# FFN1's down projection runs sub-block by sub-block, and the mixer's first buffers move to the upper part of the shared region

## The reference, cut to what matters

```
def layer_forward(x, ...):            # x: prompt 2048 x 1024, sample 128 x 1024 per core
    x = x + 0.5 * swiglu(rmsnorm(x, g1), w_gate, w_up, w_down)      # FFN1, D_FF = 2816
    h = rmsnorm(x, g2)
    u_lru, gate, u_pool = split(h @ w_in)                          # 512 + 512 + 512
    u_conv = causal_conv(u_lru, width 4);  hs = rglru(u_conv)      # gates, then a scan over time
    y = concat(gelu(gate) * hs, pool_mixer(u_pool)) ; x = x + y @ w_out
    x = x + cross_attend(rmsnorm(x, g3), mem_k, mem_v)
    x = x + 0.5 * swiglu(rmsnorm(x, g4), ...)                       # FFN2, same sizes
```

## Time and profile before

| | |
|---|---|
| runs of before | 1868.54 and 2052.18 us (median 1960.36) |
| the profiled execution | 1870.9 us, span 1869.1 us on core 1 |
| spans of the 8 cores | 1852.7 to 1869.1 us, granted clock 0.896 to 0.903 |
| TensorE (PE) busy | 1517.2 us, 81% of the span |
| VectorE (DVE), ScalarE (ACT), GpSimd (POOL) busy | 697, 509, 254 us |
| POOL's DMA queue | 142.36 MB written, 68.9% of 16 engines' span |

### The profile page before, as it was taken

One profiled execution on the slowest core, in us unless ns is written; L12 is line 12 of the kernel. 1 busy time (PEld: TensorE's weight loads), 2 busy tenths in 40 slices (PEclk: granted clock), 3 DMA queues, 4 the chain that ended last, 5 costly groups with the idle time before them and its releaser, 6 DMA issues.

```text
span 1869.1 us, 23927 instructions; the slowest of 8 cores (1852.7 to 1869.1 us)
## 1 busy us (share of the span) xinstructions
PE 1517.2 (81%) x8564; PEld 761.6 (41%) x8564; DVE 696.9 (37%) x1121; ACT 508.5 (27%) x914; POOL 253.5 (14%) x305
## 2 busy tenths in 40 slices
PE   4799997548868999886999998475675589999975
PEld 3344443225323444344455554133334444555334
DVE  3312116665275121145322114767553144222223
ACT  3211114463313111133111112573433332111111
POOL 4011101002000112210011100011102100112220
PEclk8899999778989999998999999797796599999996
DMA  9376956577913779994355953597949933558996
GB/s 173 39 82 70 108 62 72 56 96 95 134 50 41 76 83 86 118 185 96 46 68 69 99 60 44 58 113 82 124 59 144 166 46 46 69 68 80 126 159 110
DMA packets 344633, 166.20 MB, mean 89 GB/s; under 512 B 164787, under 2 KB 330675, under 8 KB 344502
## 3 DMA queue, kind: packets, MB, share of 16 engines
q0 software_dynamic: 337584, 142.36, 68.9%
q1 hardware_dynamic: 6934, 22.30, 3.8%
HBM read 295.54 MB, written 11.67 MB: 164 GB/s over the span
## 4 chain that ended last, share of the span: by engine, by line
PE 66%; DMA 12%; DVE 12%; ACT 5%; issue 4%; DVEq 0%; SPq 0%; ACTq 0%; POOLq 0%
PE psb L341 64%; DMA ring<-f2d 4%; DMA regA<-cv 4%; DVE regA L812 3%; DVE hT L470 2%; DVE rstd L463 2%; DMA yp<-regA 2%; DMA ring<-wq 1%; DVE regA L722 1%; DVE xT L466 1%; PE psb L916 1%; ACT hT L452 1%; DMA stg<-spool 1%; PE psb L936 1%; DMA ring<-win 1%
## 5 line engine op out<-in xcount | busy, mean ns | idle before, releaser
L341 PE MATMUL psb<-hT,ring 128*128 128x512 bf16 (+1 forms) x4960 | 948.9, 355 | 119.6 <-DVE hT L737 41.4
L341 PEld LDWEIGHTS psb<-hT,ring 128*128 128x128 bf16 x4960 | 451.5, 100 | 614.3 <-issue 166.6
L341 PE MATMUL psb<-regA,ring 128*128 128x512 bf16 (+2 forms) x1824 | 343.9, 352 | 30.6 <-DMA ring<-f2d 29.0
L572 DVE TENSOR_TENSOR regA<-sgt,psb 128x512 bf16<-128x512 f32 (+1 forms) x220 | 133.3, 608 | 492.9 <-PE psb L341 472.3
L570 ACT ACTIVATE sgt<-psb 128x512 f32<-128x512 f32 (+1 forms) x220 | 117.0, 533 | 507.4 <-PE psb L341 489.7
L341 PEld LDWEIGHTS psb<-regA,ring 128*128 128x128 bf16 x1824 | 169.4, 101 | 202.3 <-issue 40.0
L452 ACT ACTIVATE hT<-xT 128x512 bf16<-128x512 f32 (+1 forms) x200 | 103.2, 558 | 462.4 <-DVE xT L584 300.6
L584 DVE SCALAR_TENSOR_TENSOR xT<-psb,xT 128x512 f32<-128x512 f32 (+1 forms) x80 | 48.7, 610 | 273.1 <-PE psb L341 273.1
L470 DVE SCALAR_TENSOR_TENSOR hT<-xT,gains_s,rstd 128x512 bf16<-128x512 f32 (+1 forms) x160 | 96.3, 665 | 1.9 <-DVE rstd L463 0.7
L463 DVE RECIPROCAL rstd<-rstd 128x512 f32<-128x512 f32 (+1 forms) x25 | 71.7, 2869 | 47.4 <-ACT rstd L461 47.4
L327 POOL DMA_DIRECT2D ring<-f2d x40 | 53.7, 1343 | 197.1 <-PE psb L341 153.1
(11 more groups left out here) (151 smaller groups left out, 925.4 us busy)
## 6 DMA issues: line engine op xcount, KB each, us to landing
ring<-f2d POOLq DMA_DIRECT2D x40, 704.0 KB, 27.7
ring<-win POOLq DMA_DIRECT2D x30, 512.0 KB, 8.1
ring<-f1g POOLq DMA_DIRECT2D x22, 512.0 KB, 9.0
ring<-f1u POOLq DMA_DIRECT2D x22, 512.0 KB, 10.1
ring<-f1d POOLq DMA_DIRECT2D x16, 704.0 KB, 12.5
ring<-f2g POOLq DMA_DIRECT2D x22, 512.0 KB, 7.0
ring<-f2u POOLq DMA_DIRECT2D x22, 512.0 KB, 7.7
ring<-wout POOLq DMA_DIRECT2D x20, 512.0 KB, 8.7
```

Source lines behind the costliest of these rows:

```text
L341: last = e.matmul(out_ap, l, r, start=(i == 0), stop=(i == n - 1))
L572: P.add("dve", lambda e, t=t, bu=bu, Wd=Wd, f=f, c0=c0: e.tensor_tensor(a_bf[:, f, c0:c0 + Wd], sgt[t][:, 0:Wd], psb[bu][:, 0:Wd], ALU.mul ...
```

## The change

FFN1 gets `sb_outer=True`, as FFN2 has. The mixer's `uL`, `uP` and gate buffers move above word 12672 and from then on read "RB" alone; the other mixer buffers move down to words 0 to 11295. The mixer's barrier is split into two memsets: one for "RB", one for "RA". Both carry a scheduler cost of 0.1.

```
-        def ra_barrier(rb=True, phase=None):
+        def ra_barrier(rb=True, phase=None, write_rb=True):
...
-            P.add("dve", lambda e: e.memset(bar[:, 0:1], 0.0), writes=["RA", "bar"] + (["RB"] if rb else []))
+            if rb and not write_rb:
+                P.add("dve", lambda e: e.memset(bar[:, 1:2], 0.0), writes=["RB", "bar1"], cost=0.1)
+            P.add("dve", lambda e: e.memset(bar[:, 0:1], 0.0), writes=["RA", "bar"] + (["RB"] if (rb and write_rb) else []), cost=0.1)
...
-            ra_barrier(phase="mixer")
+            ra_barrier(phase="mixer", write_rb=False)
             Hc, Hp = 3, 15
             def uLv(c):
-                return ra_f32(c * 528, nseq * (Hc + L)).rearrange("p (s t) -> p s t", s=nseq)
+                return ra_f32(12672 + c * 528, nseq * (Hc + L)).rearrange("p (s t) -> p s t", s=nseq)
             def uPv(g):
-                return ra_f32(2112 + g * 528, nseq * (Hp + L)).rearrange("p (s t) -> p s t", s=nseq)
+                return ra_f32(14784 + g * 528, nseq * (Hp + L)).rearrange("p (s t) -> p s t", s=nseq)
...
-            GA, CV, TA, TB, MM = (4224 if sbi % 2 == 0 else 19456), 6272, 8320, 10368, 12416
+            GA, CV, TA, TB, MM = (16896 if sbi % 2 == 0 else 18944), 0, 2048, 4096, 6144
...
                         P.add("act", lambda e, cc=cc, src3=src3: e.copy(uLv(cc)[:, :, Hc:Hc + L], src3),
-                              reads=[PS(b), "RA", ("uLh", cc)], writes=[("uL", cc)])
+                              reads=[PS(b), "RB", ("uLh", cc)], writes=[("uL", cc)])
...
-            ffn("f1", sbs)
+            ffn("f1", sbs, sb_outer=True)
```

More of the change, by code:

```diff
@@ L601, in f3 @@
                 return f2(base, c).rearrange("p (s t) -> p s t", s=nseq)
-            GA, CV, TA, TB, MM = (4224 if sbi % 2 == 0 else 19456), 6272, 8320, 10368, 12416
+            GA, CV, TA, TB, MM = (16896 if sbi % 2 == 0 else 18944), 0, 2048, 4096, 6144
             def cvbv(c):
-                return ra_bf16(14464 + c * 256, 512)[:, 0:Wd]
+                return ra_bf16(8192 + c * 256, 512)[:, 0:Wd]
             def psv(i):
-                return ra_f32(15488 + i * 528, nseq * (Hp + L)).rearrange("p (s t) -> p s t", s=nseq)
+                return ra_f32(9216 + i * 528, nseq * (Hp + L)).rearrange("p (s t) -> p s t", s=nseq)
             def dlv(g):
-                return ra_bf16(16544 + g * 256, 512)[:, 0:Wd]
+                return ra_bf16(10272 + g * 256, 512)[:, 0:Wd]
             R4 = range(4)
@@ L615, in mixer_sb @@
                     P.add("dve", lambda e, c=c: e.tensor_copy(uLv(c)[:, 0, 0:Hc], cL[:, c, :]),
-                          reads=["RA", ("cL", c), ("uL", c)], writes=[("uLh", c)])
+                          reads=["RB", ("cL", c), ("uL", c)], writes=[("uLh", c)])
                     P.add("dve", lambda e, c=c: e.tensor_copy(uPv(c)[:, 0, 0:Hp], cP[:, c, :]),
-                          reads=["RA", ("cP", c), ("uP", c)], writes=[("uPh", c)])
+                          reads=["RB", ("cP", c), ("uP", c)], writes=[("uPh", c)])
                 else:
                     P.add("dve", lambda e, c=c: e.tensor_copy(uLv(c)[:, :, 0:Hc], sc_hist[:, c, :].rearrange("p (s r) -> p s r", s=16)),
-                          reads=["RA", ("sc_hist", c), ("uL", c)], writes=[("uLh", c)])
+                          reads=["RB", ("sc_hist", c), ("uL", c)], writes=[("uLh", c)])
                     P.add("dve", lambda e, c=c: e.tensor_copy(uPv(c)[:, :, 0:Hp], sp_hist[:, c, :].rearrange("p (s r) -> p s r", s=16)),
-                          reads=["RA", ("sp_hist", c), ("uP", c)], writes=[("uPh", c)])
+                          reads=["RB", ("sp_hist", c), ("uP", c)], writes=[("uPh", c)])
             for j in (0, 1, 4, 5, 2, 3):
@@ L633, in mixer_sb @@
                         P.add("act", lambda e, cc=cc, src3=src3: e.copy(uLv(cc)[:, :, Hc:Hc + L], src3),
-                              reads=[PS(b), "RA", ("uLh", cc)], writes=[("uL", cc)])
+                              reads=[PS(b), "RB", ("uLh", cc)], writes=[("uL", cc)])
                     elif cc < 8:
                         P.add("act", lambda e, cc=cc, b=b: e.activation(f2(GA, cc - 4), psb[b][:, 0:Wd], AF.Gelu_apprx_tanh),
-                              reads=[PS(b), "RA"], writes=[("ga", sbi % 2, cc - 4)])
+                              reads=[PS(b), "RB"], writes=[("ga", sbi % 2, cc - 4)])
                     else:
                         P.add("act", lambda e, cc=cc, src3=src3: e.copy(uPv(cc - 8)[:, :, Hp:Hp + L], src3),
-                              reads=[PS(b), "RA", ("uPh", cc - 8)], writes=[("uP", cc - 8)])
+                              reads=[PS(b), "RB", ("uPh", cc - 8)], writes=[("uP", cc - 8)])
                 if j == 1:
@@ L655, in mixer_sb @@
                             P.add("dve", lambda e, c=c: e.tensor_copy(cL[:, c, :], uLv(c)[:, 0, L:L + Hc]),
-                                  reads=["RA", ("uL", c)], writes=[("cL", c)])
+                                  reads=["RB", ("uL", c)], writes=[("cL", c)])
                     fill(1)
@@ L661, in mixer_sb @@
                             P.add("dve", lambda e, c=c: e.tensor_copy(cP[:, c, :], uPv(c)[:, 0, L:L + Hp]),
-                                  reads=["RA", ("uP", c)], writes=[("cP", c)])
+                                  reads=["RB", ("uP", c)], writes=[("cP", c)])
                     for g, win in enumerate((2, 4, 8, 16)):
```

## The result

The changed kernel takes 1917.3 us (median of 11 runs), the kernel before, beside it on the same chip, 1872.4 us (10 runs). The ratio is **1.0236, with a 95% interval of 1.0203 to 1.0269**: slower, by about 44 us. The profiled execution took 1926.3 us, its slowest core (core 3) spans 1924.7 us.

A forecast was written before the change was run, and what follows sets the result against it. The prediction took PE, with 66% of the chain, to bound the kernel, and FFN1's DMA slack to be spent. Its terms 19.7 + 4.7 + 29.6 − 9.3 = +44.7 on 1870.9 gave 1916 us, own range 1905 to 1934, wider 1888 to 1950.

The forecast's parts named there:

- The price of a slab: Down-phase loads: each reloaded slab takes 6.24 us, read from FFN2 in pass 0, against PE's 4.75 us.
- Pass 0 up to `wout`: Pass 0, down phase and `win`: 16 slabs in place of 8, PE stands 17 us for `win`; +19.7 us.
- so I take offsets from them directly: Both passes: FFN2's slab times from its down phase's start apply to FFN1, as ring, queue and work ahead match.
- Norm of sub-block 1: Pass 0, between `wout` and the next `win`: reciprocal and scalings now stand on DVE behind four `wout` additions; +4.7 us.
- Pass 1 up to `wout`: Pass 1, down phase and `win`: 24 slabs in place of 8, last slab at +124; +29.6 us.
- +151.5: Pass 1: the time after the down phase's start at which `win` ends, +121.9 before.
- Pass 1, sub-block 1: Pass 1: two `win` slabs fill part of the wait before `wout`, their convolution runs beside `wout`; −9.3 us.
- At nothing: Second memset, new addresses, all later stages and POOL's 24 more issues: claimed to cost no time.
- That loads hide: Both passes, down phases: slabs come within PE's 4.75 us, so not slower; 1849 us, chance 7%.
- The faster queue (1898): Both passes: slabs at 5.06 us everywhere, faster but not enough; 1898 us, chance 23%.
- The worst queue: Both passes: slabs at 7.3 us each; 1965 us, chance 15%.

The follow-up runs named there:

- move only: The changed kernel with FFN1's down slabs loaded once per pass as before, keeping only the moved buffers and split barrier; ratio 1.000 to the kernel before.
- wide ones: The changed kernel with FFN1 down slabs of 11 chunks of 256 columns in place of 22 of 128, same bytes; ratio 0.995 to the kernel before.

## Why the prediction came out as it did

The direction, the mechanism and the time (1916 for a measured 1917.3) held. That the time was met this closely is luck: the four terms missed by −7.4, +3.5, +5.3 and +1.7 us, and these errors cancel to +3.1, less than cores and runs differ among themselves. Against the median of 1960 us that was shown, 1916 would have been 2% less, and the kernel became 2.4% slower; the prediction says that it forecasts against 1870, and only from the other base is its direction wrong. By its own steps:

- **The price of a slab**, 6.24 us, taken from FFN2. Means over the eight cores of the changed kernel: in pass 0 slab 7 lands at +33.7 and slab 15 at +81.8, 6.0 us each; in pass 1 slab 7 lands at +31.9 and slab 23 at +129.7, 6.1 us each. The size is right, between the price by bytes (5.9) and 6.24.
- **Pass 0 up to `wout`, +19.7: measured +12.3.** The mechanism stood (PE waits for `win` with down slabs in the ring, the barrier comes with the last group), the size was off, and the step that failed is "so I take offsets from them directly". From FFN2's offsets the last slab was put at +86.5 and the first `win` slab at +91. They land at +81.8 and +84.5 (means of the eight cores), and the down phase ends at +111.3 in place of +117.9, which is 6.6 of the 7.4 us. On core 3 the wait was 13.3 us and not 17, the barrier at 324.7 and not near 330. FFN1 has no better start than FFN2: in the changed kernel itself slabs 7 to 13 of pass 0 land at +33.7 to +72.3 in FFN1 and at +33.8 to +73.1 in FFN2. Only then do they part: slabs 14 and 15 land at +76.2 and +81.8 in FFN1, at +81.3 and +92.9 in FFN2. Beside these last slabs FFN2 stores four output tiles and loads four input tiles, in the kernel before from +67 and +81 on, and FFN1 does neither:

```profile
811.45 13.96 SPq L946 DMA_DIRECT2D yp<-regA  x4
825.56 3.47 SPq L905 DMA_DIRECT2D regA<-xp  x4
```

  The prediction took this traffic off in pass 1 and not in pass 0. That it is what delays FFN2's two slabs fits these rows; no run takes it away, so it is not shown.
- **Norm of sub-block 1, +4.7: measured +8.2.** The order on DVE and the waits were as told; the sum lacked the lower granted clock of the `win` behind them (0.89 in place of 1.00, 2.2 us).
- **Pass 1 up to `wout`, +29.6: measured +34.9.** The mis-sized part is the last slab: put at +124, FFN2's +126.9 less 3 us for its stores, it lands at +129.7 (+126 to +136). The first 17 slabs came as in FFN2 of before (slab 16 at +90.1, there +91.4), the last seven 5.7 us apart, there 4.9 (all means of the eight cores). The prediction read 4.7 us a slab there, but the 131 GB/s of that window make 5.5 us for 721 KB. Why the tail is slower here is open; six `win` slabs stand behind it in the queue, and none in FFN2. The prediction had 6.24 throughout as the top of its own range. (The parts of its +151.5 add up to 151.2.)
- **Pass 1, sub-block 1, −9.3: measured −7.6.** Two `win` slabs ran ahead of `wout` as told.
- **At nothing:** the moved buffers and the second memset cost nothing, shown by move only. Of the later stages, FFN2's two down phases took 102.1 and 127.1 us before and take 101.4 and 129.1 us now (means of the eight cores); the rest was not followed.
- **Rivals.** That loads hide is refuted for this shape of slab, and nearly true for wide ones, whose 134 to 144 GB/s let 512-column sub-blocks through. The faster queue (1898) described pass 0 in part, pass 1 not at all. The worst queue is out: no down phase of FFN1 came near 7.3 us a slab.

The Trainium skill, "HBM Reference", section Specifications (TRN2) (the prediction names the section Access), gives about 358 GB/s to a core when both of a pair stream. No down phase shown here came near it: twice 144 GB/s, in the best of these windows, is 288 read.

## What to carry to other kernels

A loop that loads its weights again for each sub-block is priced by the phase of the same kernel that already does so, but such a phase must be read for what else moves beside it, and on more than one core: here FFN2's last slab of pass 0 lands 11 us later than FFN1's in the same kernel, after the same start. When a load gets late, ask which instruction the engine's fixed list puts next and what ready work stands behind it: here a planner that believed in a faster queue made a wait of 13 us out of nothing, and one number took it back. Before reloading, look at what the ring still holds: keeping six of eight slabs turned the change from 2.4% slower to level, and to 1.8% faster with FFN2 done the same way, of which most is to be had in FFN2 without this change.

## What the runs showed of the hardware

- The rate of POOL's casting loads depends on the length of the runs: 512-byte runs 115 to 128 GB/s written (405552 packets in all), 1024-byte runs 134 to 144 (349232), and 26.9 against 10.8 us from issue to landing.
- Short waits cost more than themselves: after waits of 1.5 and 4.4 us the next 96 matmuls took 23.5 us at a granted clock of 0.89, in place of 21.3 us at 1.00.
- The last two slabs of FFN2 in pass 0, with four output and four input tiles moving beside them, land 5 and 11 us later than the same slabs of FFN1 in the same kernel (+81.3 and +92.9 against +76.2 and +81.8); the slabs before them land together.
